# A hybrid diffusion step on one core: the merge stages turn the branch in another order

## The reference, cut to what matters

```
proj = h @ lw['w_in']                      # m_g: its last 3 * D_MODEL columns
branches = jnp.stack([o_ret, o_diff, o_gdn], axis=2)
merged = jnp.einsum('blnw,nwd->blnd', branches, lw['w_branch'])
gates = jax.nn.sigmoid(m_g.reshape(B, L, N_BRANCH, D_MODEL))
m = jnp.sum(gates * merged, axis=2) @ lw['w_out']
```

## Time and profile before

| | us |
|---|---|
| median of 3 executions | 4743.91 |
| lowest and highest | 4742.27 and 4745.16 |
| the profiled execution | 4743.94 |
| its span | 4742.1 |
| TensorE busy in it | 4033.1 (85%) |
| VectorE, ScalarE, GpSimd busy | 2862.9, 1452.5, 1713.5 |

### The profile page before, as it was taken

How to read it: one execution, slowest core, us unless ns; L and a number is a source line. 1 busy time by engine, 2 the same in 40 slices (tenths; PEclk the granted TensorE clock), 3 DMA queues, 4 the chain that set the end, 5 groups by cost and what they waited for, 6 DMA issues and landing times. The chain is left out here.

```text
span 4742.1 us, 62627 instructions
## 1 busy us (share of the span) xinstructions
PE 4033.1 (85%) x20680; PEld 3324.5 (70%) x20680; DVE 2862.9 (60%) x5850; ACT 1452.5 (31%) x2898; POOL 1713.5 (36%) x1392
## 2 busy tenths in 40 slices
PE   6888788687979959999878887886878899599998
PEld 4567487566778848888645664775666788588886
DVE  4112548565168996678941134485652698966698
ACT  4333433222231122224343334332223311222244
POOL 2245154332532303344432441543334333033453
PEclk8999998797989999999989999987979899999999
DMA  5333231000328819999753332310013288299997
GB/s 194 108 124 108 89 115 65 15 6 20 119 90 295 330 72 339 354 355 365 293 175 117 116 117 98 108 63 5 6 36 120 91 311 296 83 352 357 357 369 278
DMA packets 335074, 819.36 MB, mean 173 GB/s; under 512 B 29548, under 2 KB 109500, under 8 KB 332732
## 3 DMA queue, kind: packets, MB, share of 16 engines
q1 hardware_dynamic: 258772, 530.74, 31.7%
q0 software_dynamic: 73728, 268.47, 15.1%
q10 hardware_dynamic: 2304, 16.78, 0.9%
HBM read 791.15 MB, written 24.74 MB: 172 GB/s over the span
## 5 line engine op out<-in xcount | busy, mean ns | idle before, releaser
L298 POOL TENSOR_TENSOR weight_ring_low<-weight_ring,weights_high 128x512 fp32r<-128x512 f32 x608 | 824.5, 1364 | 1330.3 <-ACT weights_high L270 1329.4
L2090 PE MATMUL bank<-work,weight_ring 128*128 128x256 f32 x4096 | 905.2, 379 | 1.6 <-ACT gates_z L2187 1.6
L2090 PEld LDWEIGHTS bank<-work,weight_ring 128*128 128x128 f32 x4096 | 778.8, 190 | 109.6 <-issue 1.9
L270 ACT ACTIVATE weights_high<-weight_ring 128x512 fp32r<-128x512 f32 x672 | 414.6, 630 | 791.6 <-PE bank L323 538.5
L322 PE MATMUL bank<-weights_high,h_features_high 128*128 128x512 f32 x960 | 387.5, 404 | 57.4 <-POOL weight_ring_low L298 35.5
L2106 PE MATMUL bank<-expert_low,expert_gates_split 128*128 128x512 f32 x1024 | 401.5, 392 | 0.0
L323 PE MATMUL bank<-weights_high,h_features_low 128*128 128x512 f32 x960 | 382.6, 399 | 0.0
L326 PE MATMUL bank<-weight_ring_low,h_features_high 128*128 128x512 f32 x960 | 382.1, 398 | 0.0
L322 PEld LDWEIGHTS bank<-weights_high,h_features_high 128*128 128x128 f32 x960 | 185.6, 193 | 111.8 <-POOL weight_ring_low L298 61.5
L339 PE MATMUL bank<-h_features_high,weights_high 128*128 128x384 f32 x640 | 227.0, 355 | 41.6 <-POOL weight_ring_low L298 37.2
L1216 DVE SCALAR_TENSOR_TENSOR work<-work 128x390 f32<-128x390 f32 x288 | 255.7, 960 | 0.0
(11 more groups left out here) (406 smaller groups left out, 8210.9 us busy)
## 6 DMA issues: line engine op xcount, KB each, us to landing
weight_ring<-in_peer_u_columns_dram SPq DMA_DIRECT2D x256, 512.0 KB, 6.1
weight_ring<-in_peer_v_dram SPq DMA_DIRECT2D x256, 512.0 KB, 5.9
weight_ring<-in_w_in_dram SPq DMA_DIRECT2D x208, 512.0 KB, 5.4
weight_ring<-in_w_mod_dram SPq DMA_DIRECT2D x32, 1024.0 KB, 5.2
weight_ring<-in_w_branch_dram SPq DMA_DIRECT2D x48, 512.0 KB, 6.7
weight_ring<-in_w_mod_dram SPq DMA_DIRECT2D x32, 512.0 KB, 6.6
weight_ring<-in_peer_wq_dram SPq DMA_DIRECT2D x32, 512.0 KB, 5.6
merged<-gate_matrix_rest SPq DMA_DIRECT2D x32, 512.0 KB, 7.8
```

The lines of the kernel that those rows point to most:

```text
L270: nc.scalar.activation(WH[:, k % HIGHS, :], RW[:, j, k, :], ACT.Copy).then_inc(s["high"], 1)
L298: ops.tensor_tensor(RWL[:, j, k, :], RW[:, j, k, :], WH[:, k % HIGHS, :].bitcast(F32), ALU.subtract)\
L2090: mm = nc.tensor.matmul(PS[4 + p % 2][:, b * DENSE:(b + 1) * DENSE], UR[:, q % RB, k * P:(k + 1) * P], HTF[:, k, :], start=(k == 0), stop= ...
```

## The change

It touches the merges alone. The semaphore `ready` is gone. TensorE turns five of the six banks at the start, now banks 3 to 7, and goes straight to the first gate product; the sixth (tile 2, upper half of the features) is turned behind that product, into bank 6, once the low part that was made from that bank's earlier content is there. The first branch product waits for five low parts at its first step and for the sixth at its fifth step. ScalarE splits the first four steps of the gate chunk first, then takes five turned banks, goes on with the chunk, and takes the sixth turned bank ahead of the first sigmoid. The four products on TensorE are no longer a loop in hardware; they are written out one behind the other.

The two helpers that make the high and the low parts (`act_turned_high`, `dve_turned_low`) only get the tiles and the banks as arguments; their instructions are the same.

```diff
-        def act_split(act, s, base, chunks, use, more=False, loop=True):
+        def act_split(act, s, base, chunks, use, more=False, loop=True, begun=lambda: None):
...
             if base == 0:
                 act_high(act, s, 0, 0, 0, range(HIGHS))
+            begun()
...
+            turn_banks = (3, 4, 5, 6, 7, 6)
+            late = 2 * TILES - 1
...
                     pe_start(pe, s)
-                    pe_transpose_tokens(pe, H, s["ready"], s["turned"])
-                    pe.wait_ge(s["turned_low"], 2 * TILES)
-                    pe_project(pe, s, ((HTH, HTL), (OTH, OTL)), 2 * chunks, 0,
-                               lambda i, j: (s["branch_banks_free" if j else "gate_banks_free"], i + 1), s["done"])
+
+                    def turn(n):
+
+                        t, b = divmod(n, 2)
+                        for k in range(4):
+                            kk = 4 * b + k
+                            mm = nc.tensor.transpose(PS[turn_banks[n]][:, k * P:(k + 1) * P], H[:, t, kk * P:(kk + 1) * P], ID)
+                        mm.then_inc(s["turned"], 1)
+
+                    def product(i, j, xh, xl):
+
+                        pe.wait_ge(s["branch_banks_free" if j else "gate_banks_free"], i + 1)
+                        for k in range(KT):
+                            if j and i == 0 and k in (0, 4):
+                                pe.wait_ge(s["turned_low"], late + k // 4)
+                            pe.wait_ge(s["low"], KT * (2 * i + j) + k + 1)
...
+                        pe.drain().then_inc(s["free"], 1)
+
+                    for n in range(late):
+                        turn(n)
+                    for i in range(chunks):
+                        product(i, 0, HTH, HTL)
+                        if i == 0:
+                            pe.wait_ge(s["turned_low"], 4)
+                            turn(late)
+                        product(i, 1, OTH, OTL)
...
                     act.sem_inc(s["gate_banks_free"], 1)
-                    act_turned_high(act, OTH, s)
...
                         if j == 1:
                             return
+                        if i == 0:
+                            act_turned_high(act, OTH, s, tiles=(late,), banks=turn_banks)
                         act.wait_ge(s["used"], i + 1)
...
-                    act_split(act, s, 0, 2 * chunks, use)
+                    act_split(act, s, 0, 2 * chunks, use,
+                              begun=lambda: act_turned_high(act, OTH, s, tiles=range(late), banks=turn_banks))
...
-                    dve.sem_inc(s["ready"], TILES)
                     dve.sem_inc(s["branch_banks_free"], 1)
                     dve.sem_inc(s["used"], 1)
-                    dve_turned_low(dve, OTH, OTL, s)
+                    dve_turned_low(dve, OTH, OTL, s, banks=turn_banks)
```

More of the change, by code:

```diff
@@ L362, in build, with act_turned_high @@
         HTF = BIG[:, 0:KT * DEC_SEQ].rearrange("p (k n) -> p k n", k=KT)
-        def act_turned_high(act, dst, s, full=False):
-            for n in range(2 * TILES):
+        def act_turned_high(act, dst, s, full=False, tiles=range(2 * TILES), banks=range(2 * TILES)):
+            for n in tiles:
                 act.wait_ge(s["turned"], n + 1)
@@ L370, in act_turned_high, with dve_turned_low @@
                                          ACT.Copy)
[L371 removed]
+                nc.scalar.activation(features_view(dst, n), PS[banks[n]].rearrange("p (k n) -> p k n", k=4), ACT.Copy)\
                     .then_inc(s["turned_high"], 1)
[L374 to L375 removed]
+        def dve_turned_low(dve, high, low, s, tiles=range(2 * TILES), banks=range(2 * TILES)):
+            for n in tiles:
                 dve.wait_ge(s["turned_high"], n + 1)
[L377 removed]
+                nc.vector.tensor_tensor(features_view(low, n), PS[banks[n]].rearrange("p (k n) -> p k n", k=4),
                                         features_view(high, n).bitcast(F32), ALU.subtract).then_inc(s["turned_low"], 1)
@@ L1710, in stage_merge @@
             s = signals(STREAM + "gate_banks_free branch_banks_free done"
-                        " turned turned_high turned_low ready gate used chain ahead small")
+                        " turned turned_high turned_low gate used chain ahead small")
             GT = BIG[:, 0:TILES * CHUNK].rearrange("p (t n) -> p t n", t=TILES)
@@ L1733, in _ @@
                     pe_start(pe, s)
-                    pe_transpose_tokens(pe, H, s["ready"], s["turned"])
-                    pe.wait_ge(s["turned_low"], 2 * TILES)
-                    pe_project(pe, s, ((HTH, HTL), (OTH, OTL)), 2 * chunks, 0,
-                               lambda i, j: (s["branch_banks_free" if j else "gate_banks_free"], i + 1), s["done"])
+                    def turn(n):
[10 more added lines that the diff above has]
+                            pe.wait_ge(s["low"], KT * (2 * i + j) + k + 1)
+                            for t in range(TILES):
+                                rows, out = slice(t * P, (t + 1) * P), PS[3 * j + t]
+                                nc.tensor.matmul(out, xh[:, k, rows], WH[:, k % HIGHS, :], start=(k == 0), stop=False)
+                                mm = nc.tensor.matmul(out, xl[:, k, rows], WH[:, k % HIGHS, :], start=False, stop=False)
+                                if t == TILES - 1:
+                                    mm.then_inc(s["high_free"], 1)
+                                mm = nc.tensor.matmul(out, xh[:, k, rows], RWL[:, j, k, :], start=False, stop=(k == KT - 1))
+                                if k == KT - 1:
+                                    mm.then_inc(s["done"], 1)
+                        pe.drain().then_inc(s["free"], 1)
[7 more added lines that the diff above has]
+                        product(i, 1, OTH, OTL)
                 @block.gpsimd
```

4 lines of the change are left out of this document (removed).

## The result

| | before | changed |
|---|---|---|
| median of 6 executions each, us | 4742.07 | 4723.82 |
| lowest and highest | 4737.38 to 4745.16 | 4719.69 to 4731.46 |
| span of the profiled execution | 4742.1 | 4719.1 |

The ratio is 0.9965, 95% interval 0.9954 to 0.9977: the change makes the kernel 16.6 us faster (11 to 22). The prediction had the direction right and the size too small: 11.2 us were forecast, and 4723.8 us lies under the range, which ended at 4726. Of the 8.9 us between the forecast 4732.7 and 4723.8, 1.8 lie in the kernel before itself: its median was 4743.9 us in the three executions that the forecast started from and is 4742.1 in the six here.

What follows compares the result with a forecast made beforehand. TensorE was taken as the bound inside a merge, so an earlier start shortens the stage. The terms -9.6 - 2.7 + 2.8 - 1.7 = -11.2 us took 4743.9 to 4732.7 us, range 4726 to 4740 us.

Steps and rivals of the forecast that it cites:

- Step 1: Start of each merge: ScalarE splits gate weights when they land, so the gate product starts sooner; -9.6 us.
- Step 2: Boundaries between TensorE's products: straight code removes the loop's jump, 0.45 us once in each merge; -2.7 us.
- Step 3: Four late transposes between first gate and first branch product, paid in full on TensorE; +2.8 us (2.6 to 5.1).
- Step 4: TensorE's clock behind the first gate matmul: one merge of six avoids its slow stretch; -1.7 us, bounds -10 to +10.
- case (c): Merge starts: the full clock is kept in three or more merges; at best 4726 us; chance 0.13.
- (b): Merge starts: gate product begins at 1.2 GHz, second slow stretch in about three of six merges; 4739.5 us; chance 0.22.
- (d): Gate product: ScalarE's splits and banks only change places, TensorE starves for the fifth step; 4744 us; chance 0.05.
- (f): Branch product: waits for the sixth low part behind the table load, 2 us per merge; 4745 us; chance 0.02.
- (e): TensorE's longer straight code: instruction fetches make a hole in each merge, 23.4 us; 4756 us; chance 0.03.

Runs made afterwards that it cites:

- the one with the banks first: Changed kernel with ScalarE taking the five turned banks before the gate weights again; ratio to the kernel before 0.9981, median 4730.9 us.
- two banks late: Changed kernel with two banks turned behind the first gate product instead of one, 16 transposes at the start; ratio to before 0.9993, median 4735.1 us.

## Why the prediction was wrong, step by step

**Step 1 was right.** -9.6 us were put down, the traces give -10.0 and -9.3. The first split is at the landing, the gate product 2.1 us behind it (2.02 assumed; the straight code alone also starts it 0.1 us later), and no step of the gate product starves.

**Step 2 was right.** -2.7 us were put down. The jumps gave 3.1, since three of the six were dearer than the one that was read, and the straight code alone gives 2.7 in its trace.

**Step 3 was too dear.** +2.8 us (2.6 to 5.1) against 6 x 0.27 = +1.6, under the lower bound. The length of four transposes at full clock was right (0.46 taken, 0.43 measured), but part of them lies under the pause that a boundary has in any case. I had added them to that boundary instead of asking what of it they replace.

**Step 4 failed.** It took one merge in six as kept, -1.7 us. The two traces of the changed kernel have five and three, at 1.6 us each -8.0 and -4.8 us. The step named both effects, a shorter idle stretch and fewer transposes, and let them cancel, as if each merge stood at the old odds. The runs show what each is worth: with 2.55 to 2.70 us of idle no merge keeps the clock (18 of 18 lose it in the two traces of before and in the one with the banks first), with more work put ahead of the gate product all do (24 of 24 in four traces), with 1.39 to 2.41 us 10 of 18 do, those with the shorter stretches; and with four transposes fewer none does. The change moved the start from the first group into the third. The chance for case (c), 0.13, should have been the largest, and its lower end, 4726 us, took four further kept clocks from a sum that had counted the late transposes 1.2 us too dear and started from a median 1.8 us too high. With the measured terms, -10.0 - 3.1 + 1.6 and between three and five clocks, the sum is -16.3 to -19.5 us; the ratio says -16.6. How many merges keep the clock in an execution that was not profiled is not known.

**The rivals.** (b) did not happen in the changed kernel's two traces, and did with two banks late. (d) and (f) did not: no engine waits for the fifth step or the sixth low part. (e) is the one that I had mispriced in kind. No hole on TensorE goes with a fetch of instructions in these traces; where one falls beside the weights' transfers, these land up to 1.1 us later, and step 1 has put them on the path. In the changed kernel's two traces none falls there (the profile has 148 of them instead of 142). The prediction had no reason for that, so it was luck; with eight more transposes some 3 us were lost that way.

On the rule of the Trainium skill ("TensorE: Matmul & The Clock Gate", Part 4) that transposes don't count for the clock: the trace after speaks against it again. In the first merge the engine had done nothing but 20 transposes since 255.9, and the clock was 1.00 from 267.0 on. The rows list them as MATMUL and do not name a mode; that they are what the rule means is taken from the kernel's `nc.tensor.transpose`.

## What to carry to other kernels

When a change moves an idle stretch ahead of matmuls, look at the granted clock behind it before and ask on which side of the old idle time the new one lies; here shortening 2.6 us by 0.7 to 0.9 us on average was worth 5 to 8 us, beside the 9 to 10 us that the earlier start gave directly. An idle stretch that has to stay can be filled with matmuls into a bank whose content is not needed, few in number and not longer than the wait; 20 transposes did it in the kernel before, two wide matmuls in the changed one. And when a wait for an engine is removed so that a transfer becomes the last thing to arrive, everything that delays that transfer is now on the path.

## What the runs showed of the hardware that I had not expected

- With a transfer of 16 KB of instructions (2.42 MB in 148 on queue q8) in the first 4 us of a merge, SP's four issues took 2.9 to 3.8 us instead of 2.1 to 2.5, and the weights landed after 4.2 to 4.9 us instead of 3.6 to 4.2, 10 times in 10. That the queue is TensorE's is inferred from its count: 142 before, 143 with 20 transposes more, 148 with straight code on TensorE alone, and still 142 with ScalarE's order changed. The Trainium skill, "Runtime: NRT & Kernel Launch", section "Instruction fetch mechanics", calls such a fetch mostly hidden; for TensorE it was, for the weights it was not. Why SP's own issues take longer is not shown by these traces.
- A stage whose code doesn't change has two lengths, some 300 and some 293.5 us, with mean granted clocks of 0.82 and 0.85. Comparing two single traces end to end would have credited 6.6 us of that to the change.
- 16 transposes (3.65 us at half clock) with 2.27 us of idle behind them left the clock at 0.50 for another 5.8 us of dense matmuls; 20 (4.5 us) with 1.55 us behind them did not, and 20 with 2.64 us did once, for 5.3 us.
- In the 18 merges with 20 transposes ahead and 1.39 to 2.41 us of idle, 1.79 us and less kept the clock at 1.00 and 1.82 us and more lost it; behind 28 transposes 2.31 us kept it.
